# A solver round moved behind the value tiles, spare products inside the 64-row rounds, and an earlier forget product in a long one-core model kernel

## The chip, the cores and the metric

One core of a Trainium2 chip. The metric is the device time of one launch in microseconds (us), the median of the runs of a kernel. Everything is fp32.

## What is computed

A token sequence of 256 goes through two blocks of a model with D = 1024. Cut to what matters here:

```python
# first block: two layers; each: x += .5*norm(swiglu); x += norm(mixer); x += .5*norm(swiglu)
#   layer 0's mixer is an attention + state-space mixer, layer 1's is the RWKV-7 time mix
# second block, 16 meta tokens ahead of the 256, two of these "hybrid" layers:
def hybrid_layer(h, ...):
    u = rms_norm(h, norm_g)
    dq, dk, dv, dz, fq, fk, fv, fz, f_logit = split(u @ w_in)
    q1, q2, k1, k2 = rope(dq), ..., rope(dk), ...
    p = softmax(q1 k1) - lam * softmax(q2 k2)          # differential heads
    log_f = log_sigmoid(f_logit + b_forget); cum = cumsum(log_f)
    s = fq fk * scale + cum[query] - cum[key]          # forgetting heads
    return h + (concat(o_a * silu(dz), o_b * silu(fz)) @ w_out)
```

The RWKV time mix runs in two chunks of 128 tokens. Inside a chunk and a head it needs the inverse of a unit lower-triangular 128x128 matrix for each of 16 heads and 2 chunks. The 32x32 diagonal blocks are inverted on VectorE; the off-diagonal ones follow by products: one round that joins 32-blocks to 64-blocks, one that joins these to 128.

## The kernel before, in words

All engines run programs written out by hand in order; the order of issue on an engine is the order of the Python code, and semaphores tie the engines together. `product_pe`, `ffn_pe` and the projections are TensorE products of 128x128 weights; a helper `group` (line 277) issues the matmuls of one accumulation. In the trace each fp32 matmul is two MATMUL records. PSUM banks 0 to 3 are taken in turn by `turn_d` (VectorE empties them and raises `dve_out`), banks 4 to 7 by `turn_a` (ScalarE empties them, `act_out`); a turn n waits until turn n - 4 has been emptied. Weights come through a ring of six 1 MB slots. SyncE loads them in the order of `plan_weights`; slot n is loaded once slot n - 6 is released (`slot_used`), `take_slot` waits for its arrival.

**RWKV stage** (`rwkv_pe`, `rwkv_act`, `rwkv_dve`, `rwkv_pool`). On TensorE, in order: key, rate and eight receptance tiles (`r_product`, line 277) with the four pairs of score products (`pair_scores`, L1689) set among them; g1 and four value tiles; four groups of transposes "tok" (L1787) and the bonus product; four products `g2_product(t, h)` of two 512-column matmuls each; then the solver rounds. Round "m32" (L1815, 64 products of 32x32) needs `t64`, which VectorE copies at L2215 after its 31 steps of inversion (L2204, L2206). Round "t32" (L1828, L1830, 96 products of 32x32) needs m32 as emptied by VectorE (L2227, L2228) and the block-diagonal matrices `tts`, one copied by VectorE (L2221, `sc_dve` 2), one by ScalarE (L2054, `sc_act`). Rounds "m64" and "t64" (L1839, L1848) are 32 products of 64x64 each, in four groups of eight; each group is emptied by VectorE in 0.68 us. Then two small transposes `bonus_rows` (L1801), a drain, four full-array products of the identity with 512 columns of constants into one bank that nobody reads, and `chunk_pe`, the recurrence (L1896 to L1929). ScalarE empties tok, then g2 (`gtk`, L2049), then copies `tts[1]`.

**Hybrid stages** (`hybrid_pe` and its fellows). 32 feature tiles p = 0 to 31 in the order `FT`: dq0, dq1, dk0, dk1, dv0, dv1, dq2, ... Attention units (scores L2487, transposes L2499, value product L2513) are worked off from p = 5 on, one step of a unit beside each tile. ScalarE copies a tile out (L2542), GpSimd issues four DMAs per q or k tile that swap its halves (L2692, two buffers), VectorE does the rotation (L2632 to L2634) at step p + 2, and raises `roped`. A transpose of a value tile (L2472) waits until VectorE has copied the one before (L2639). At p = 11 TensorE does the forget product (8 columns, 16 records); VectorE adds the bias at step 11, ScalarE takes the logarithm at step 12, VectorE scans at step 13 (L2608). GpSimd, whose queue has all eight rotations ahead of it, then writes the sums to DRAM (L2694), reads them back to all partitions (L2696) and adds the masks (L2700). The first forgetting unit's scores need that.

**Mixer of layer 0** (`mixer_pe`). At p = 5 TensorE transposes the compressed probabilities (L1167), which VectorE has ready at L1552; ScalarE copies them (L1340) at its step 5. The first value product at p = 6 waits for that copy (`pct_done`).

```python
                    if u == 0:
                        pe.wait_ge(pct_done, 1)
```

Of the kernel before, what the change touches and what calls it, by code (L numbers as in the profile page):

```python
# [11 lines left out]
P = 128  # L12
S = 256
T = S // P
# [100 lines left out]
def plan_weights(d):  # L115
# [70 lines left out]
def model_kernel(nc, d, out, stop=None):  # L186
    ctx = ExitStack()
    with ctx:
# [853 lines left out]
        def mixer_pe(pe):  # L1042
# [74 lines left out]
            for p in range(STEPS):  # L1117
# [18 lines left out]
                if p == 2:  # L1136
# [26 lines left out]
                if p == 5:  # L1163
                    pe.wait_ge(pc_done, 1)
                    for t in range(T):
                        for g in range(2):
                            m = nc.tensor.transpose(ps[:, 7, (2 * t + g) * P:(2 * t + g + 1) * P],  # L1167
                                                    pcmp[:, t, 4 * g:4 * g + 4, :].rearrange("p h n -> p (h n)"), ident)
                    m.then_inc(pct_ready, 1)
# [108 lines left out]
        def mixer_act(act):  # L1278
# [35 lines left out]
            for p in range(STEPS):  # L1314
# [23 lines left out]
                if p == 5:  # L1338
# [320 lines left out]
        def rwkv_pe(pe):  # L1659
# [121 lines left out]
            s = S_V + 4  # L1781
            pe.wait_ge(krr, 3 * KD)
# [25 lines left out]
            g2_product(1, 1)  # L1808
            pe.wait_ge(sc_dve, 1)
            for t in range(T):  # L1810
                n = turn_d("m32", t)
                for h in range(SH):
                    ch = SH * t + h
                    for g in range(2):
                        m = nc.tensor.matmul(bank_d(n)[64 * g + 32:64 * g + 64, 32 * h:32 * h + 32],  # L1815
                                             at0[:, ch, :] if g == 0 else at64[64:96, ch, 32:64], t64[64 * g:64 * g + 32, ch, 0:32],
                                             start=True, stop=True, skip_group_check=True)
                m.then_inc(to_dve, 1)
            pe.wait_ge(sc_dve, 2)
            pe.wait_ge(sc_act, 1)  # L1820
            for t in range(T):
# [1001 lines left out]
```

## Time and profile before

| | us |
|---|---|
| median of 3 runs (1753.21 to 1759.9) | 1757.9 |
| the profiled execution, its time | 1766.56 |
| its span, first to last instruction | 1764.4 |
| TensorE busy in it | 1699.5 |
| granted TensorE clock, mean over the span | 0.984 |

Stages in the span: feed-forward 0 to 225, mixer 225 to 420, its output and two feed-forwards 420 to 870, RWKV stage 870 to 1130 (with its output product), feed-forward 1130 to 1340, hybrid 0 from 1340 to 1560, hybrid 1 from 1560 to the end. A clock of 1.00 in a row is 2.4 GHz, 0.50 is 1.2 GHz; a value between them is a stretch with some of each. Idle time in square brackets stands ahead of the instruction, with what ended it.

### The profile page before, as it was taken

Reading aid. Unit: us, or ns where it says so; the run is one execution under the profiler, and the core shown is the slowest. Engines: PE = TensorE matmul, PEld = TensorE weight load, DVE = VectorE, ACT = ScalarE, POOL = GpSimd, SP = SyncE. Lnnn points to the kernel's source line nnn. Section 1 sums busy time; section 2 is a strip of 40 time slices with the busy share of each in tenths; the row PEclk is TensorE's granted clock in tenths of the full one; section 3 lists DMA queues with packets and bytes.
Section 4 is the critical chain, followed back from the end, with each engine's and each line's share of the span. In section 5 each row is a group of like instructions: output and inputs, shape, how many; then the busy total and the mean of one; then the engine's idle time right before and its main releaser. Section 6 shows DMA issues by size and latency. Waiting matters only on the chain.

```text
span 1764.4 us, 26355 instructions
## 1 busy us (share of the span) xinstructions
PE 1699.5 (96%) x10798; PEld 1329.2 (75%) x10798; DVE 1033.8 (59%) x2001; ACT 420.3 (24%) x1049; POOL 260.0 (15%) x339
## 2 busy tenths in 40 slices
PE   8999999999999999999998999999998999999898
PEld 7997487775799749996476778699846777467674
DVE  5777435752577737776588647387754555325353
ACT  2000124532200002000157213201102344123431
POOL 3334000000022201221004040022201120011100
PEclk9999999999999999999999979999999999999999
DMA  8666744213454554545533300355557763468630
GB/s 263 216 210 206 170 109 138 73 53 107 132 176 159 191 169 141 178 157 191 143 103 119 120 25 2 98 189 165 176 144 150 119 119 106 79 108 120 118 111 24
DMA packets 196967, 237.27 MB, mean 134 GB/s; under 512 B 28300, under 2 KB 177216, under 8 KB 196592
## 3 DMA queue, kind: packets, MB, share of 16 engines
q1 hardware_dynamic: 191872, 224.97, 45.9%
q0 software_dynamic: 4960, 10.61, 1.9%
q8 instruction: 87, 1.43, 0.3%
q14 instruction: 32, 0.26, 0.0%
q10 hardware_dynamic: 16, 0.00, 0.0%
HBM read 232.30 MB, written 1.07 MB: 132 GB/s over the span
## 4 chain that ended last, share of the span: by engine, by line
PE 86%; DVE 6%; ACT 3%; DMA 2%; issue 2%; POOL 0%; POOLq 0%; SPq 0%; DVEq 0%; ACTq 0%
PE ps L589 28%; PE ps L277 23%; PE ps L655 14%; PE ps L518 6%; PE ps L599 3%; PE ps L1879 2%; DMA arena<-arena 1%; PE ps L2487 1%; PE ps L2499 1%; PE ps L2518 1%; PE ps L335 1%; DMA cum_rows<-arena 1%; PE ps L2513 1%; PE ps L1896 1%; PE ps L1702 0%
## 5 line engine op out<-in xcount | busy, mean ns | idle before, releaser
L277 PE MATMUL ps<-hT,ring 128*128 128x272 f32 (+4 forms) x1696 | 365.1, 372 | 4.3 <-ACT hT L359 4.0
L277 PEld LDWEIGHTS ps<-hT,ring 128*128 128x128 f32 (+1 forms) x1696 | 292.1, 193 | 59.6 <-issue 7.8
L589 PE MATMUL ps<-arena,ring 128*128 128x128 f32 x1280 | 162.6, 275 | 0.0
L655 PE MATMUL ps<-ring,arena 128*128 128x512 f32 x352 | 155.9, 593 | 1.7 <-DVE more L760 1.7
L850 POOL TENSOR_TENSOR arena<-arena 128x128 f32<-128x128 f32 x44 | 36.7, 833 | 793.4 <-DVE arena L774 449.7
L589 PEld LDWEIGHTS ps<-arena,ring 128*128 128x128 f32 x1280 | 152.6, 192 | 0.0
L589 PE MATMUL ps<-hT,ring 128*128 128x128 f32 x1280 | 150.1, 275 | 0.0
L589 PEld LDWEIGHTS ps<-hT,ring 128*128 128x128 f32 x1280 | 146.5, 192 | 0.0
L655 PEld LDWEIGHTS ps<-ring,arena 128*128 128x128 f32 x352 | 66.6, 190 | 87.1 <-issue 87.1
L589 PE MATMUL ps<-arena 128*128 128x128 f32 x960 | 120.3, 275 | 0.0
L589 PEld LDWEIGHTS ps<-arena 128*128 128x128 f32 x960 | 113.6, 192 | 0.0
L711 ACT ACTIVATE gains<-ps 128x512 f32<-128x512 f32 x40 | 23.9, 597 | 353.9 <-PE ps L589 353.9
L518 PE MATMUL ps<-ring,arena 128*128 128x512 f32 (+1 forms) x192 | 84.5, 596 | 0.7 <-ACT arena L2550 0.7
L783 DVE TENSOR_TENSOR gains<-gains,ps 128x256 f32<-128x256 f32 x40 | 16.8, 420 | 95.3 <-ACT gains L711 95.3
L518 PEld LDWEIGHTS ps<-ring,arena 128*128 128x128 f32 (+1 forms) x192 | 32.6, 174 | 50.1 <-issue 48.7
L2692 POOL DMA_DIRECT2D arena<-arena x64 | 31.4, 498 | 262.6 <-ACT arena L2542 238.7
L741 DVE TENSOR_TENSOR ring<-ring 128x512 f32<-128x512 f32 x80 | 70.1, 915 | 0.0
L655 PE MATMUL ps<-arena 128*128 128x512 f32 x144 | 65.8, 593 | 0.0
L599 PEld LDWEIGHTS ps<-hT,ring 128*128 128x128 f32 x512 | 60.4, 199 | 4.5 <-issue 4.3
L589 PE MATMUL ps<-hT,arena 128*128 128x128 f32 x480 | 63.4, 275 | 0.0
L599 PE MATMUL ps<-hT,ring 128*128 128x128 f32 x512 | 61.3, 283 | 2.0 <-DMA ring<-in_ffn_w_gate 1.5
L794 DVE TENSOR_TENSOR gains<-gains,ps 128x384 f32<-128x384 f32 x80 | 44.3, 554 | 27.0 <-PE ps L589 25.6
(488 smaller groups left out, 2720.4 us busy)
## 6 DMA issues: line engine op xcount, KB each, us to landing
ring<-in_ffn_w_gate SPq DMA_DIRECT2D x44, 1024.0 KB, 5.4
ring<-in_ffn_w_up SPq DMA_DIRECT2D x44, 1024.0 KB, 7.2
ring<-in_ffn_w_down SPq DMA_DIRECT2D x44, 1024.0 KB, 4.9
ring<-in_w_in SPq DMA_DIRECT2D x32, 1024.0 KB, 10.3
ring<-in_ab_w_in SPq DMA_DIRECT2D x12, 1024.0 KB, 5.3
ring<-in_w_out SPq DMA_DIRECT2D x8, 1024.0 KB, 5.0
ring<-in_ab_w_out SPq DMA_DIRECT2D x6, 1024.0 KB, 4.8
ring<-in_c_w_k SPq DMA_DIRECT2D x4, 1024.0 KB, 6.5
```

The lines of the kernel that those rows point to most:

```text
L277: last = nc.tensor.matmul(o, l, r, start=(i == 0), stop=(i == len(pairs) - 1))
L335: m = nc.tensor.transpose(ps[:, b + k // 4, (k % 4) * P:(k % 4 + 1) * P], xn[:, t, k * P:(k + 1) * P], ident)
L518: m = nc.tensor.matmul(o[:, h, :], lhs(k, t), slot2(n)[:, k % 2, h * 512:(h + 1) * 512], start=(k == 0), stop=(k == nk - 1))
L589: m = nc.tensor.matmul(o, left[:, k, :], right[:, k, :], start=(k == 0), stop=(k == 3))
L599: m = nc.tensor.matmul(ps[:, 4 + w, 256 * i + P * t:256 * i + P * (t + 1)], slot8(s0 + w)[:, k, i * P:(i + 1) * P], hT[:, k, h_cols(t)], s ...
L655: return nc.tensor.matmul(ps[:, BANK[i], :], hid[p][:, left, :], right, start=(p == 0), stop=(p == LAST))
L711: nc.scalar.activation(gu_e[:, :, 1:6:4], gu_a[:, :, 0:2], ACT.Copy).then_inc(a_copied, 1)
L741: nc.vector.tensor_tensor(w_part(n + w, 1, 0), w_part(n + w, 0, 0), w_part(n + w, 1, 0), ALU.subtract).then_inc(w_sums, 1)
L794: nc.vector.tensor_tensor(gu_e[:, w, 1:4], gu_e[:, w, 1:4], gu_b[:, w, 0:3], ALU.add).then_inc(b_taken, 1)
L850: nc.gpsimd.tensor_tensor(hid[q][:, 4], hid[q][:, 1], hid[q][:, 3], ALU.add).then_inc(hid_sums, 1)
L1879: m = nc.tensor.matmul(ps[:, 2 * t + h, :], yT[:, k, t * P:(t + 1) * P], slot2(s + k // 2)[:, k % 2, h * 512:(h + 1) * 512], start=(k == 0 ...
L2692: nc.gpsimd.dma_start(rth[to, (n - 1) % 2, fc], fmh[of, QK[kind] + i, fc]).then_inc(rot_in[(n - 1) % 2], 16)
```

## The change

**Mixer.** The transposes of the compressed probabilities go from the end of step 5 to the start of step 6, ahead of that step's scores; ScalarE's copy from step 5 to step 6.

**RWKV.** The receptance products come one earlier against the score products, on TensorE and on ScalarE. Round m32 is issued right behind the value tiles, and VectorE empties it before it makes `tts[0]`; ScalarE copies `tts[1]` ahead of emptying g2. Round t32 stands ahead of the last g2 product. A full-array product whose result nobody reads stands ahead of each of the eight groups of rounds m64 and t64; the four behind the rounds are gone.

**Hybrids.** The forget product and its chain on ScalarE and VectorE are four steps earlier (7, 8, 9), its weights stand fifth in the plan. The tile order begins dq0, dk0, dq1, dk1, and the first units wait for two rotations, not three; the first two slots are both released at p = 4. One activation table with both logarithm and exponential is loaded at the start of the stage.

```diff
 # plan_weights
-        for c in (0, 2, 4, 1, 3, 5, None, 8, 10, 12, 9, 11, 13, 6, 7, 14, 15):
+        for c in (0, 2, 4, 1, None, 3, 5, 8, 10, 12, 9, 11, 13, 6, 7, 14, 15):
 # mixer_pe, ahead of the scores of step p (behind them, with p == 5, before)
+                if p == 6:
+                    pe.wait_ge(pc_done, 1)
+                    for t in range(T):
+                        for g in range(2):
+                            m = nc.tensor.transpose(ps[:, 7, (2 * t + g) * P:(2 * t + g + 1) * P],
+                                                    pcmp[:, t, 4 * g:4 * g + 4, :].rearrange("p h n -> p (h n)"), ident)
+                    m.then_inc(pct_ready, 1)
 # mixer_act
-                if p == 5:
+                if p == 6:
                     act.wait_ge(pct_ready, 1)
 # rwkv_pe
-            for j in range(4):
+            for j in range(5):
                 r_product(j)
             pair_scores(0)
-            r_product(4)
+            r_product(5)
             pair_scores(1)
-            r_product(5)
+            r_product(6)
             pair_scores(2)
-            r_product(6)
+            r_product(7)
             pair_scores(3)
-            r_product(7)
...
             s = S_V + 4
+            pe.wait_ge(sc_dve, 1)
+            for t in range(T):
+                n = turn_d("m32", t)
...
             g2_product(0, 0)
             g2_product(0, 1)
             g2_product(1, 0)
-            g2_product(1, 1)
-            pe.wait_ge(sc_dve, 1)
-            for t in range(T):
-                n = turn_d("m32", t)
...
             pe.wait_ge(sc_dve, 2)
             pe.wait_ge(sc_act, 1)
...
+            g2_product(1, 1)
+            spare = pe_a.n + 1
+            pe.wait_ge(act_out, spare - 4)
+
+            def full_array():
+                group(bank_a(spare), [(ident, cst[:, 0:512])])
+
             for t in range(T):
                 pe.wait_ge(dve_out, job["t32", t])
                 for h8 in range(2):
+                    full_array()
                     n = turn_d("m64", t, h8)
...
                     pe.wait_ge(dve_out, job["m64", t, h8])
+                    full_array()
                     n = turn_d("t64", t, h8)
...
-            n = pe_a.n + 1
-            pe.wait_ge(act_out, n - 4)
-            for i in range(4):
-                group(bank_a(n), [(ident, cst[:, 0:512])])
 # rwkv_act: key_root(6), r_out(4), decays(5), key_root(7) now ahead of scores_out(0);
 #   r_out(6) ahead of scores_out(2), r_out(7) ahead of scores_out(3);
 #   the copies of tts[1] ahead of those of gtk
 # rwkv_dve: the copies of m32 right behind those of t64, ahead of those of tts[0]
 # the hybrids
+        FT[1], FT[2] = FT[2], FT[1]
...
-                      frees=p % 2 == 0).then_inc(f_ready, 1)
+                      frees=2 if p == 4 else 1 - p % 2).then_inc(f_ready, 1)
...
-                if p == 11:
+                if p == 7:
                     take_slot(pe, s)
                     x_turn()
...
-                        pe.wait_ge(roped, 8 * layer + (3, 4, 7, 8)[i])
+                        pe.wait_ge(roped, 8 * layer + (2, 4, 7, 8)[i])
 # hybrid_act
+            nc.scalar.preload_act_table_set(LN_EXP)
-                if p == 12:
+                if p == 8:
 # hybrid_dve: p == 11 becomes p == 7 (bias), p == 13 becomes p == 9 (scan)
```

## Rows read from the trace of the kernel before

**Rows 1.** The page: engine, busy us, share of the span, instructions.

```profile
PE 1699.5 (96%) x10798; PEld 1329.2 (75%) x10798; DVE 1033.8 (59%) x2001; ACT 420.3 (24%) x1049; POOL 260.0 (15%) x339
```

**Rows 2.** Stretches of 20 us: length, busy PE, PEld, DVE, ACT, POOL; clock, DMA share, GB/s.

```profile
300.00:320.00 20.00, 18.05 (x105) 14.44 (x106) 16.32 (x34) 9.95 (x31) 0.00 (x0) 0.91 0.18 53
...
940.00:960.00 20.00, 15.72 (x96) 12.60 (x95) 14.32 (x26) 19.26 (x58) 8.32 (x10) 0.91 0.31 106
...
1020.00:1040.00 20.00, 19.15 (x181) 16.42 (x182) 9.50 (x16) 0.00 (x0) 3.54 (x2) 0.50 0.16 52
...
1360.00:1380.00 20.00, 16.07 (x71) 12.05 (x70) 7.65 (x22) 2.97 (x12) 5.37 (x11) 0.91 0.55 103
...
1660.00:1680.00 20.00, 17.16 (x81) 13.32 (x82) 10.93 (x23) 8.71 (x21) 5.89 (x2) 0.83 0.43 81
```

**Rows 3.** Timeline, RWKV scores: start, us, engine, line, operation, idle before.

```profile
945.55 1.16 PE L1689 MATMUL ps<-gains,arena 64*128 64x128 f32 x16 [2.67 <-ACT more L1960]
...
962.44 1.25 DVE L2200 STREAM_TRANSPOSE arena<-arena 128x1024 f32<-128x1024 f32 x1 [1.15 <-ACT arena L1956]
```

**Rows 4.** Timeline from the value tiles to round t32.

```profile
970.27 27.89 PE L277 MATMUL ps<-ring,arena 128*128 128x256 f32 x128
...
991.84 3.20 DVE L2215 COPY gains<-arena 32x1024 f32<-32x1024 f32 x3
...
998.01 1.91 PE L1787 MATMUL ps<-cst,arena 128*128 128x128 f32 x16
...
1003.40 8.50 PE L277 MATMUL ps<-ring,gains 128*128 128x512 f32 x16
...
1012.43 4.28 ACT L2054 ACTIVATE arena<-arena 32x512 f32<-32x512 f32 x4
...
1016.81 0.26 PE L1828 MATMUL ps<-arena,more 32*32 32x32 f32 x2 [2.77 <-ACT arena L2054]
```

**Rows 5.** The chain that ended last, rounds m64, t64 and the four spare products.

```profile
1021.81 6.70 PE ps L1839 x61
...
1028.83 6.46 PE ps L1848 x61
...
1035.71 5.88 PE ps L277 x8
```

**Rows 6.** Timeline, VectorE ahead of the recurrence.

```profile
1036.47 0.91 DVE L2248 MEMSET gains<- 128x1024 f32 x1 [0.16 <-issue]
```

**Rows 7.** Timeline, mixer steps 5 and 6.

```profile
301.95 0.66 PE L1167 MATMUL ps<-cst,arena 128*128 128x128 f32 x4 [2.66 <-DVE arena L1552]
...
308.84 0.37 ACT L1321 ACTIVATE arena<-ps 128x256 f32<-128x256 f32 x1
...
309.19 2.82 PE L277 MATMUL ps<-arena 32*64 32x128 f32 x20
```

**Rows 8.** Timeline, hybrid 0: waits of TensorE and VectorE.

```profile
1367.38 0.22 PE L2487 MATMUL ps<-arena 64*16 64x16 f32 x4 [3.93 <-DVE arena L2634]
...
1365.84 0.44 DVE L2632 TENSOR_TENSOR arena<-arena,cst 128x272 f32<-128x272 f32 x1 [6.37 <-DMA arena<-arena]
...
1405.94 0.44 DVE L2632 TENSOR_TENSOR arena<-arena,cst 128x272 f32<-128x272 f32 x1 [2.49 <-DMA arena<-arena]
...
1432.18 5.96 DVE L2648 TENSOR_TENSOR arena<-arena 128x272 f32<-128x272 f32 x1
...
1433.07 4.76 POOL L2700 TENSOR_TENSOR gains<-gains,cst 128x2176 f32<-128x2176 f32 x1
```

**Rows 9.** Timeline, hybrid 1: the chain behind the forget product.

```profile
1635.95 0.52 POOL L2694 DMA_DIRECT2D cum_rows<-arena  x1 [21.74 <-DVE arena L2608]
...
1661.28 0.46 DVE L2624 TENSOR_TENSOR arena<-ps,more 128x288 f32<-128x288 f32 x1 [13.54 <-POOL more L2700]
...
1662.84 0.85 PE L2472 MATMUL ps<-cst,arena 128*96 128x128 f32 x3 [4.49 <-DVE arena L2639]
```

**Rows 10.** A stretch in hybrid 1 behind its second wait, columns as in rows 2.

```profile
1662.90:1668.20 5.30, 5.30 (x18) 3.87 (x19) 5.23 (x7) 0.53 (x3) 2.99 (x1) 0.50 0.07 23
```

More of the change, by code:

```diff
@@ L1781, in rwkv_pe @@
             s = S_V + 4
+            pe.wait_ge(sc_dve, 1)
+            for t in range(T):
+                n = turn_d("m32", t)
+                for h in range(SH):
+                    ch = SH * t + h
+                    for g in range(2):
+                        m = nc.tensor.matmul(bank_d(n)[64 * g + 32:64 * g + 64, 32 * h:32 * h + 32],
+                                             at0[:, ch, :] if g == 0 else at64[64:96, ch, 32:64], t64[64 * g:64 * g + 32, ch, 0:32],
+                                             start=True, stop=True, skip_group_check=True)
+                m.then_inc(to_dve, 1)
             pe.wait_ge(krr, 3 * KD)
@@ L2046, in rwkv_act @@
                     nc.scalar.activation((btk, ktk)[w][:, j4 * 512:(j4 + 1) * 512], next_a(), ACT.Copy).then_inc(act_out, 1)
-            for t in range(T):
-                for h in range(2):
-                    nc.scalar.activation(gtk[:, t, h * 512:(h + 1) * 512], next_a(), ACT.Copy).then_inc(act_out, 1)
             act.wait_ge(solved, 1)
@@ L2055, in rwkv_act @@
             m.then_inc(sc_act, 1)
+            for t in range(T):
+                for h in range(2):
+                    nc.scalar.activation(gtk[:, t, h * 512:(h + 1) * 512], next_a(), ACT.Copy).then_inc(act_out, 1)
             nc.scalar.preload_act_table_set(LN_EXP)
@@ L2217, in rwkv_dve @@
                     m.then_inc(sc_dve, 1)
+            for t in range(T):
+                b = next_d().rearrange("p (h n) -> p h n", h=SH)
+                cs = slice(SH * t, SH * t + SH)
+                nc.vector.tensor_copy(m32[32:64, cs, :], b[32:64])
+                nc.vector.tensor_copy(m32[96:P, cs, :], b[96:P]).then_inc(dve_out, 1)
             dve.wait_ge(tt_zero, 3)
@@ L2223, in rwkv_dve @@
             nc.vector.tensor_copy(bsum, next_d()[64:80, 0:S]).then_inc(dve_out, 1)
-            for t in range(T):
-                b = next_d().rearrange("p (h n) -> p h n", h=SH)
-                cs = slice(SH * t, SH * t + SH)
-                nc.vector.tensor_copy(m32[32:64, cs, :], b[32:64])
-                nc.vector.tensor_copy(m32[96:P, cs, :], b[96:P]).then_inc(dve_out, 1)
             for t in range(T):
@@ L2436, in hybrid_pe @@
             for p in range(4):
-                if p % 2 == 0:
-                    take_slot(pe, s + p // 2)
+                if p < 2:
+                    take_slot(pe, s + p)
                 raw_n[FT[p]] = n = f_turn()
                 fc = slice(f_cols(layer, FT[p][0]).start, META + P)
-                group(f_bank(layer, n)[:, fc], [(slot8(s + p // 2)[:, k, (p % 2) * P:(p % 2 + 1) * P], hT[:, k, fc]) for k in range(KD)])
+                group(f_bank(layer, n)[:, fc], [(slot8(s + p % 2)[:, k, (p // 2) * P:(p // 2 + 1) * P], hT[:, k, fc]) for k in range(KD)])
             trans_pe(pe, 1)
@@ L2444, in hybrid_pe @@
             for p in range(4):
-                if p == 2:
-                    s += 1
                 fc = slice(META + P, L2)
-                group(f_bank(layer, raw_n[FT[p]])[:, fc], [(slot8(s)[:, k, (p % 2) * P:(p % 2 + 1) * P], hT[:, k, fc]) for k in range(KD)],
-                      frees=p == 2).then_inc(f_ready, 1)
-            s += 1
+                group(f_bank(layer, raw_n[FT[p]])[:, fc],
+                      [(slot8(s + p % 2)[:, k, (p // 2) * P:(p // 2 + 1) * P], hT[:, k, fc]) for k in range(KD)]).then_inc(f_ready, 1)
+            s += 2
             for p in range(4, len(FT)):
```

32 lines of the change are left out of this document (9 added, 23 removed).

## The prediction

> **What bounds the kernel.** I read the page first: TensorE is busy for 96% of the span [rows 1]. So the end moves only by what TensorE gets rid of: its own work, its idle gaps, and the time that it works at half clock. The table of 20 us stretches shows where the last two lie [rows 2]. In nearly all stretches TensorE is busy for 20 of 20 us at clock 1.00; the rows shown are exceptions, and each lies where the change works. 0.91 is 3.4 to 3.6 us at 1.2 GHz, 0.83 is 6.8 us, and from 1020 to 1040 all of it. Then I read the timeline around each exception, for what ended the wait.
>
> In the RWKV solver the chain of events is plain [rows 4]. Tok starts at 998.0, the four g2 products end at 1011.9, round m32 ends at 1014.04 (1016.81 less 2.77). Then TensorE waits 2.77 us for ScalarE, whose copy of `tts[1]` began only after g2 was emptied and took 4.28 us. In this wait, behind 2 us of 32-row products, the clock fell. It stayed at 1.2 GHz through both 64-row rounds, 13.3 us of dense work [rows 5], and rose only inside the full-array products behind them: at half clock a 512-column product takes about 1.7 us, at full clock at most 1.06 (8.50 / 8, [rows 4]), and the four took 5.88. The recurrence starts at 1041.6.
>
> **The change, part by part.** Times are against the profiled execution.
>
> *Solver.* From the start of tok (or now m32) to the recurrence, before: 1041.6 - 998.0 = 43.6 us. After, all at full clock: m32 2.1 (1014.04 - 1011.9); tok 1.9; bonus product 3.5 (1003.40 - 998.01 - 1.91); four g2 8.5; t32 3.2 (m32's 2.1 for 64 products, times 96/64); 64-row rounds half of 6.70 + 6.46, 6.6; eight spare products at 1.06, 8.5; bonus_rows and drain 0.5. The sum is 34.8. The spare product's 0.85 to 1.06: I take the g2 row, since it too changes between kinds of tile. Two changes of tile per group instead of one could add 0.1 each, 0.8 in all.
>
> Is anything late in this order? m32 needs the second copy of `t64`, 992 + 2.1 = 994, and the value tiles end at 998.0: 4 us of cover, where before 18 us of g2 and others lay between. If VectorE's inversion began 4 us later, each further us would count in full. `tts[1]` now starts on ScalarE behind tok (about 5 us in) and is done 9.3 us in; t32 comes 16 us in. VectorE empties m32 and makes `tts[0]` by 7. Each group of a round is emptied in 0.68 us beside about 1.9 of TensorE. All hidden. Ahead of the recurrence VectorE clears a state for 0.91 us, until 1037.4, 1.8 us behind bonus_rows [rows 6]; the four spare products hid that. With none behind, the first emptying comes about 0.9 late. Solver: -8.8 + 0.9 = **-7.9**, between -10.5 (spare products at 0.85, memset hidden) and -5 (changes of tile dear).
>
> *Receptance against scores.* ScalarE is the bound there, 19.26 of 20 us busy [rows 2], TensorE waits for it, 2.67 us at the most [rows 3]. Done by hand in the new order: TensorE has r_product(7), 3.5 us, ahead of its last wait and not behind it. ScalarE has one more copy and the later waits ahead of the last scores, so that VectorE's inversion starts some 1.7 us later than 962.4; the value tiles end 0.7 us earlier. So m32's 4 us of cover shrink to 1.6. I take **-0.5**, from -2.5 to +2.
>
> *Mixer.* The 2.66 us wait for VectorE at 301.95 goes [rows 7]; the tile of step 6 fills it, and the half clock behind it (0.09 of 20 us, 1.8) goes too. But ScalarE's copy is now in its step 6, behind the exponentials and the convolution's sigmoid of step 5, which wait for VectorE; its step 6 began at 308.84. The copy ends at 309.8 (308.84 + 0.37 + some 0.6 for 512 columns), and the first value product, at 309.19 before, starts there. Worked forward from the tile before, TensorE has done its scores by about 306.3 (VectorE's mask of the unit before decides) and then has nothing for 3.5 us, longer than the wait that went, so the clock falls again, now over products and a tile of some 6 us. Sum: +0.6, and 0 to +3.6 for the clock. **+2**, from +0.5 to +4. No copy or wait behind it gives it back, since TensorE is dense after.
>
> *Hybrids, first units.* TensorE waited 3.93 us in hybrid 0 for the third rotation [rows 8] and a little less in hybrid 1; each was followed by 3.4 us of half clock. VectorE in turn waited 6.37 for its DMA. With two rotations needed, the score product goes ahead, but the third rotation is as late as it was, and VectorE's order has it ahead of the first unit's mask and of the copy of the first value tile, for which TensorE waits one tile later (by about 2.4 us). The earlier forget product, 3.6 us, is moved, not added. The later wait for it, 0.7, goes. The step 11 rotation also came by a late DMA, at 1405.94; TensorE, now 3 us ahead, would run into it. And both first slots are released together, so 2 MB of weights are in the queues when the third rotation is issued. I take **-2.5** and **-1**, from -5 to +3 each.
>
> Of this the Trainium skill, "DMA: Bandwidth & Descriptors", section "Queues, rings and completion order", says that each engine takes turns between queues at the granularity of a packet. By that rule a small rotation DMA would hardly wait for a ring load, and both terms would be at their good end, about -5. The 6.37 us wait disagrees as far as it goes.
>
> *Hybrid 1, bias.* The chain from the scan takes 1661.2 - 1635.95 = 25 us [rows 9], and VectorE waits 13.54 for it. Four steps earlier (about 5 us each, 32 tiles in some 160 us), and with GpSimd's eighth rotation issued by 1614.2 (1635.95 less 21.74), it starts some 20 us sooner, so the 13.54 are covered with 6 or more to spare. TensorE's 4.49 go, and the half clock behind it, 5.3 us of dense work at half rate, 2.7 [rows 10]. **-7.2**, from -8 to -5.
>
> *Bias additions elsewhere.* GpSimd's 4.76 us held VectorE's L2648 up to 5.96 us where its like takes 0.44 [rows 8]. They fall 20 us earlier now, beside units of the differential heads in both hybrids. In hybrid 0 this cost a TensorE gap of about 2 us and half clock before, and will again. In hybrid 1 it is new, in a looser stretch. **+1**, from 0 to +4.
>
> The skill, "SBUF — State Buffer", section "Who interferes with whom", says that a VectorE instruction with two SBUF inputs waits for a GpSimd one that reads SBUF to its end. The row agrees. It speaks against the move: the whole 4.76 us and more of stall in each hybrid, the +4 end.
>
> *Tables.* The table loads inside the hybrids fall away. ScalarE is 24% busy over the span [rows 1], no TensorE wait shown ends on one. 0.
>
> Sum: -7.9 - 0.5 + 2 - 2.5 - 1 - 7.2 + 1 = -16.1. The profiled execution, 1766.6, is 8.7 above the median; 1750.5 there is **1742** on the median's scale.
>
> **Rivals.**
>
> *Stalls move (0.24).* The late DMAs and VectorE's order hold TensorE in both hybrids: +2.5 and +1 in place of -2.5 and -1 would be net +7 on the sum, the mixer at +4, 2 more. -16.1 + 9 = -7: 1751. For it: every wait there ends on a DMA whose landing is not moved. Against: hybrid 1's bias gap is large and simple.
>
> *The solver gains half (0.08).* m32, with 1.6 us of cover, waits for `t64`, and tile changes cost 0.2 a piece: -4 in place of -7.9: 1746, and with part of the first rival 1750.
>
> *Slower: the clock falls in t32 and nothing lifts it (0.06).* The trace has it fall behind 32-row work and not rise through 13.3 us of 64-row work [rows 5]. If t32's 3.2 us between g2 products let it fall, g2 costs 2.1 more, the rounds 6.6 more, the spare products 5 to 7 more: +14.7, which alone only gives 1757. But with no dense block behind, the recurrence begins at half clock; if its first 26 us are done so, they add up to 22: 1779. It decides from there: up to the recurrence it is no change, beyond it slower. Against: full-array products stand in each group, and the clock held through 8.5 us of g2 and m32 before the idle wait.
>
> **How the numbers follow.** Likeliest 0.62, own range 1735 to 1750; the rivals as above. 0.5% is 8.8 us, about what a measurement of this kernel can tell: faster below 1749.1, slower above 1766.7. Faster: nearly all of the first case, 0.60, a quarter of the second, half of the third: 0.69. Slower: the clock case and a little: 0.07. Same 0.24. The range leaves out the clock case and the ends: 1733 to 1756.
>
> **What the profile would show.** Clock 1.00 all through the solver, no wait ahead of L1828, 35 us from value tiles to recurrence, and about 1 us ahead of the first L1908. The mixer's gap moves from L1167 to the first value product. In hybrid 1 no wait for L2700; some gap at the second L2472 of each hybrid. The prediction is wrong if the clock dips in t32, if the rotations land later than before, or if spare products and rounds take over 18 us.

## The result

The changed kernel takes **1781.5 us** (1779.3 to 1781.9), the kernel before 1757.9: slower by 1.1%, ratio 1.0108 [1.0076, 1.0141]; the two medians by themselves would give 1.3%, inside that interval. The forecast was faster, 1742, with at most 1756. What came is close in time to the rival to which I gave 0.06 (1779), and its first half is what happened; its second half, a recurrence begun at half clock for 26 us, did not in the profiled execution. That the two times agree is therefore luck: mixer and hybrids, slower than that sum had them, made up for it.

### The profile after

The page first, then the 20 us stretches that answer to [rows 1, 2]. Columns: stretch, its length, busy time of TensorE, its weight loads, VectorE, ScalarE and GpSimd, granted clock, DMA share, GB/s.

```profile
PE 1711.2 (96%) x10806; PEld 1330.9 (75%) x10806; DVE 1036.0 (58%) x2001; ACT 394.6 (22%) x1029; POOL 260.1 (15%) x339
```

```profile
300.00:320.00 20.00, 15.07 (x75) 12.11 (x75) 13.12 (x30) 9.65 (x31) 0.00 (x0) 0.83 0.17 53
940.00:960.00 20.00, 14.26 (x77) 11.54 (x76) 17.39 (x29) 15.59 (x47) 11.06 (x14) 0.87 0.27 84
1000.00:1020.00 20.00, 18.67 (x337) 11.08 (x336) 8.70 (x14) 8.60 (x12) 1.80 (x1) 0.99 0.22 73
1020.00:1040.00 20.00, 19.91 (x114) 10.47 (x114) 4.37 (x7) 1.88 (x2) 0.00 (x0) 0.50 0.01 2
1040.00:1060.00 20.00, 19.74 (x107) 12.83 (x105) 5.85 (x11) 0.00 (x0) 2.56 (x2) 0.50 0.10 31
1380.00:1400.00 20.00, 12.31 (x53) 8.31 (x50) 6.13 (x20) 2.32 (x11) 3.25 (x7) 0.83 0.90 153
1600.00:1620.00 20.00, 11.99 (x52) 8.68 (x52) 7.66 (x20) 2.78 (x11) 1.96 (x4) 0.83 0.94 156
1660.00:1680.00 20.00, 20.00 (x102) 15.57 (x101) 11.60 (x22) 5.61 (x18) 7.56 (x2) 1.00 0.77 166
```

TensorE is as busy as before, 96%, but busy longer: 11.7 us more. The eight spare products and four taken away can't explain that at full clock. The stretch at half clock is now two rows of 20 us where it was one. The hybrids' sore points have moved: the last row, hybrid 1's wait for the sums, is whole and at full clock, as forecast, and two new rows near 1390 and 1610 have lost 8 us each.

By stage, from the starts of the same products in the two traces (spans 1764.4 and 1777.5): mixer +3.4 us, scores +1.5, value tiles to recurrence +10.4 (43.5 to 53.9), recurrence +1.2, hybrid 0 -0.4, hybrid 1 -3.1: 13.0. That is against a profiled execution of before that stood 8.7 above the median of its runs. The profiled execution of after is 2.2 us below the median of its runs, so the timed difference, 19 us by the ratio and 23.6 by the medians, is larger than the 13 of the profiles.

TensorE through the solver, to be held against [rows 4, 5]:

```profile
1020.09 0.26 PE L1826 MATMUL ps<-arena,more 32*32 32x32 f32 x2 [1.42 <-issue]
1020.98 4.08 PE L277 MATMUL ps<-ring,gains 128*128 128x512 f32 x4
1024.99 2.08 PE L277 MATMUL ps<-cst 128*128 128x512 f32 x2
1026.99 1.97 PE L1845 MATMUL ps<-gains,hT 64*64 64x64 f32 x16
...
1052.29 2.07 PE L277 MATMUL ps<-cst 128*128 128x512 f32 x2
1054.29 1.97 PE L1855 MATMUL ps<-arena,gains 64*64 64x64 f32 x16
...
1059.70 1.00 PE L1911 MATMUL ps<-arena 128*128 128x64 f32 x4
...
1061.50 0.66 PE L1911 MATMUL ps<-arena 128*128 128x64 f32 x4
```

The wait for ScalarE at t32 is gone. In its place, near the end of t32's 192 records, TensorE stops for 1.42 us, from 1018.7, for nothing that an engine did ("issue"). Just as it stopped a 16 KB block came in on the queue that carries instructions, alone on the DMA engines:

```profile
q8 instruction: 1, 0.02, 1.3%
```

It began at 1017.9 and took 1.0 us; TensorE went on 1.2 us behind its landing. All thirteen kernels whose profile has such a stop agree: it lasts 0.44 to 2.18 us, and TensorE goes on 1.2 to 1.5 us behind the landing of a block, in the kernel before as well. That TensorE ran out of instructions and waited for this block is inferred from that, not shown. The clock fell at 1019.5, in the stop. From there each g2 product, spare product and round runs at half rate: a spare product 2.0 from start to start, a group 1.9, eight times 3.9. None of the eight full-array products lifted the clock, nor did all of them together. It rose at 1060.4, 3.6 us into the recurrence: the same four products take 1.00 us before and 0.66 behind.

Mixer and scores, for [rows 7] and [rows 3]; each wait is followed by 6.8 us at half clock:

```profile
303.61 0.60 PE L1153 MATMUL ps<-cst,arena 128*128 128x128 f32 x4
305.69 0.72 PE L1167 MATMUL ps<-arena 64*128 64x128 f32 x8 [1.48 <-DVE arena L1508]
309.85 5.07 PE L277 MATMUL ps<-arena 32*64 32x128 f32 x20 [3.44 <-ACT arena L1340]
```

```profile
953.57 1.16 PE L1689 MATMUL ps<-gains,arena 64*128 64x128 f32 x16 [4.31 <-DVE gains L2195]
```

Hybrid 0, for [rows 8]: TensorE, then VectorE's third rotation, GpSimd's issue of its transfers, and SyncE's loads:

```profile
1391.65 0.85 PE L2474 MATMUL ps<-cst,arena 128*96 128x128 f32 x3 [7.69 <-DVE arena L2642]
```

```profile
1388.05 0.44 DVE L2635 TENSOR_TENSOR arena<-arena,cst 128x272 f32<-128x272 f32 x1 [11.82 <-DMA arena<-arena]
```

```profile
1372.88 1.96 POOL L2695 DMA_DIRECT2D arena<-arena  x4 [1.26 <-ACT arena L2545]
```

```profile
1372.77 8.37 SPq L308 DMA_DIRECT2D ring<-in_w_in  x3
```

The third rotation's transfers were issued 0.1 us behind a 1 MB load and landed 15.2 us later, where it was 8.3 before [rows 8]: 1365.84 less 1357.57, the latter GpSimd's issue in the trace of before. A second 1 MB load went out at 1373.2, among these transfers. Hybrid 1 shows the same with 8.0 us of wait.

### The profile page after: what moved, and what is told of

It reads as the page before. It is cut to its first block, busy times and chain, and to the rows that moved or that the text cites. A ratio compares the mean times of both kernels' runs of the same rounds, so it can differ in the third digit from the quotient of the medians.

```text
span 1777.5 us, 26346 instructions
## 1 busy us (share of the span) xinstructions
PE 1711.2 (96%) x10806; PEld 1330.9 (75%) x10806; DVE 1036.0 (58%) x2001; ACT 394.6 (22%) x1029; POOL 260.1 (15%) x339
## 4 chain that ended last, share of the span: by engine, by line
PE 88%; DVE 6%; ACT 2%; DMA 2%; issue 1%; POOL 0%; SPq 0%; DVEq 0%; ACTq 0%
PE ps L589 28%; PE ps L277 25%; PE ps L655 14%; PE ps L518 6%; PE ps L599 3%; PE ps L1882 2%; DMA arena<-arena 2%; PE ps L2489 1%; PE ps L2501 1%; PE ps L2520 1%; PE ps L335 1%; PE ps L2515 1%; PE ps L1899 1%; PE ps L1702 0%; DMA ring<-in_ffn_w_gate 0%
## 5 line engine op out<-in xcount | busy, mean ns | idle before, releaser
L277 PE MATMUL ps<-hT,ring 128*128 128x272 f32 (+4 forms) x1696 | 358.4, 367 | 4.3 <-ACT hT L359 4.0
L277 PEld LDWEIGHTS ps<-hT,ring 128*128 128x128 f32 (+1 forms) x1696 | 287.2, 190 | 58.0 <-issue 8.1
```

What stands on the lines that cost most here:

```text
L277: last = nc.tensor.matmul(o, l, r, start=(i == 0), stop=(i == len(pairs) - 1))
```

## The experiments

Ratios are to the kernel before on the same chip, whose median was 1760 to 1761 in all sets. Where the executions of a kernel fall into two groups, the ratio lies nearer to that of the means than to that of the medians.

### Which part cost what

**a_rwkv, a_hybrids, b_mixer, d_scores**: the kernel before with one part of the diff alone. d_scores takes from the RWKV part only the order of receptance and scores.

> The kernel before with the RWKV part of the change alone (order of receptance and scores, m32 early, t32 ahead of the last g2, spare products inside). By the two profiles that stage grew by 13.1 us: 1.5 in the scores, 10.3 from value tiles to recurrence, 1.2 in the recurrence's first products at half clock. If the parts don't touch one another, this kernel is 13 us slower than before (1.0075). Rival: part of it came from the stage's later start behind the mixer (3.4 us); then it is 8 us or less.

> The kernel before with the hybrid part of the change alone. By the two profiles hybrid 0 is 0.4 us shorter and hybrid 1 3.1 us, so the time falls by 3.5 us (0.998), with a wait of nearly 8 us for the third rotation at the second value tile of both. Rival: these waits were made by the phase at which the stage began; then they are 4 us or less here, and the time falls by 10 us.

> The kernel before with the mixer part of the change alone. By the two profiles TensorE's wait of 2.66 us ahead of the transposes became one of 3.44 at the first value product, with 6.8 us at half clock behind it for 3.4: 3.4 us slower up to the mixer's output. Theory: that is its whole effect, 3 to 4 us slower (1.002). Rival: the wait is taken back later in the mixer where TensorE waits for others; then no difference.

> The kernel before with the new order of receptance and score products alone. By the two profiles it costs 1.5 us up to the value tiles (a wait of 4.3 us in place of 2.7, 6.8 us at half clock in place of 3.4, less 0.75 and 0.85 of smaller waits). Nothing behind it takes that back: 1 to 2 us slower. Rival: the later start of VectorE's inversion costs nothing either, so it is within 1 us of before.

```
            median us   ratio to before
a_rwkv      1774.3      1.0078 [1.0049, 1.0108]
b_mixer     1765.6      1.0024 [1.0008, 1.0040]
a_hybrids   1764.5      1.0014 [0.9997, 1.0031]
d_scores    1760.8      1.0004 [0.9982, 1.0025]
```

The three parts sum to 1.0116, the change measured 1.0108: they account for all of it. The RWKV part is two thirds of the loss. The profiled execution of a_rwkv shows how deep it can go: t32's stop, 1.44 us, and behind it the clock low through the rounds and through the whole first half of the recurrence, until 1101.3.

```profile
1015.21 0.22 PE L1826 MATMUL ps<-arena,more 32*32 32x32 f32 x2 [1.44 <-issue]
```

```profile
1016.00:1101.00 85.00, 84.74 (x416) 65.75 (x417) 21.34 (x46) 8.53 (x26) 17.86 (x8) 0.50 0.04 13
```

That execution took 1792.9 us, the others 1770.6 to 1775.6. The mixer behaves as its profile said. The scores' 1.5 us can't be told from nothing. The hybrids' part, which by the profiles gains 3.5, does not gain in the timed runs. Waits of 7.7 us at the second value tile stand in both hybrids here too, so they don't come from the stage's start time.

### What fells the clock, and what lifts it

**a_behind**: no product inside the rounds, four behind them again. **b_batches**: as many as in the change, but four ahead of the first 64-row group and four behind the last.

```diff
 # a_behind
-                    full_array()
...
+            for i in range(4):
+                group(bank_a(n), [(ident, cst[:, 0:512])])
 # b_batches: besides, the same lines behind g2_product(1, 1)
```

> The changed kernel without the eight full-array products inside the rounds, and with the four behind the rounds, as in the kernel before. Theory 1 (the products inside lift nothing): the clock falls in t32 as before and stays low through g2(1,1) and the rounds, 4.0 + 13.2 us, and rises inside the four behind, 5.9 us; the stretch from m32 to the recurrence is 17.5 + 4.0 + 13.2 + 0.5 + 5.9 = about 41 us instead of 53.9, the recurrence starts at full clock, and the time falls by 13 to 15 us. Rival: the 16 us that eight spare products take at half clock are not lost, because without them each group waits for VectorE to empty the one before (0.68 us and its way); then the rounds take 18 us or more and the time falls by less than 10.

> The changed kernel with its eight full-array products in two batches: four ahead of the first 64-row group, four behind the last, none inside the rounds. Theory: a full-array product among 64-row groups doesn't lift a fallen clock, four in a row do (the kernel before rose inside its four). Then the clock rises in the first batch (5.9 us), the rounds run at full clock in 6.6 us and the second batch in 4.2, and the stretch from m32 to the recurrence is 17.5 + 4.0 + 5.9 + 6.6 + 0.5 + 4.2 = about 39 us for 53.9; the time is 13 to 17 us below the changed kernel's. Rival: 64-row products bring the clock down again by themselves; then the rounds take 10 to 13 us and the second batch 5.9, 45 us or more, and the time is 5 to 9 us below.

a_behind: 1769.9 us, 1.0039 [1.0023, 1.0055], 11.6 below the changed kernel (13 to 15 expected); value tiles to recurrence 42.0 us. So spare products inside the rounds are pure cost once the clock is down. b_batches lifted the clock in the first batch as expected, and the rounds behind it stayed at full clock; the stretch took 39.8 us (39 expected). Stretches of b_batches, the last in the recurrence:

```profile
1021.00:1031.00 10.00, 8.65 (x51) 3.51 (x51) 2.77 (x5) 1.88 (x2) 0.00 (x0) 0.50 0.01 2
1031.20:1044.20 13.00, 12.89 (x142) 9.38 (x140) 6.68 (x11) 0.00 (x0) 2.73 (x2) 1.00 0.19 55
1075.60:1119.80 44.20, 44.20 (x223) 41.98 (x224) 26.80 (x68) 9.88 (x37) 0.00 (x0) 0.50 0.00 1
```

But its time is 1784.8 us, 1.0104 [1.0066, 1.0142], no better than the changed kernel: 3 of 10 executions at 1763 to 1770, 7 at 1784 to 1788. The last row is why, in the one that was profiled. Both theories missed it.

**a_split**: the changed kernel with the last g2 product between the halves of t32. **e_mix**: the changed kernel with all four g2 products spread.

```diff
 # a_split, in the loop over t of round t32
-            g2_product(1, 1)
+                if t == 0:
+                    g2_product(1, 1)
 # e_mix: g2_product(0, 0) ahead of t32, then
+                if t == 1:
+                    g2_product(0, 1)
 # and in the loop over t of round m64
+                g2_product(1, t)
```

> The changed kernel with its last g2 product issued between the two halves of round t32 and not behind both; nothing else differs. Theory 1 (the fall is t32's): in the changed kernel TensorE stopped for 1.42 us inside t32, until a 16 KB instruction transfer had landed, and the clock fell in that stop. With a 2 us product of full width in that place the stop is covered, the clock holds, and the stretch from m32 to the recurrence goes from 53.9 us to about 35; the time falls by 18 us or so, to within 0.3% of the kernel before. Rival: the clock falls anyway, one or two groups later, because eight full-array products among 64-row groups are too thin to hold it; then the stretch is 48 to 52 us and the time falls by less than 6 us.

> The changed kernel with everything as it is but the place of the four g2 products: one ahead of each half of t32, one ahead of each half of m64 (in the changed kernel three ahead of t32 and one behind it; in a_split one of them was moved between the halves). The eight products inside the rounds stay. Theory (the run of thin rounds and their waits, unbroken by other work, is what the clock fell in): the stretch from m32 to the recurrence is 35 us, as d_inside's, in all executions; the time is 17 to 22 us below the changed kernel's 1781, near the kernel before. Rival 1 (the order of receptance, or the later start of everything behind the mixer, has a part in the fall): two kinds of executions as in a_split, the median above 1770. Rival 2 (what is left above before is in mixer and hybrids): then it stays 5 to 8 us above the kernel before less 7 of the solver's gain, about 1760.

The solver came out as expected in both, 35.9 us at full clock, without the stop in t32:

```profile
1005.14:1041.01 35.87, 35.61 (x516) 20.49 (x515) 14.95 (x23) 10.51 (x14) 1.80 (x1) 1.00 0.10 31
```

The times did not. a_split: 1779.6 us, 1.0077 [1.0045, 1.0110], with 3 of 10 executions at 1762 to 1766 (one of these was profiled) and 7 at 1779 to 1783. e_mix: 1779.9 us, 1.0084 [1.0050, 1.0118], one of 6 at 1763.9, five at 1779 to 1782. My theory of a_split, that t32 is the only place of a fall, fell with it, and so did that of e_mix, that the run of thin rounds is. The profiled execution of e_mix is one of the five, and shows the place: TensorE's wait where the recurrence passes from the first chunk to the second, and the stretches around it.

```profile
1071.04 0.74 PE L1909 MATMUL ps<-gains 128*128 128x128 f32 x2 [1.08 <-DVE arena L2259]
```

```profile
1020.00:1040.00 20.00, 19.74 (x162) 11.63 (x162) 5.78 (x11) 2.20 (x3) 0.09 (x1) 1.00 0.00 1
1071.20:1115.50 44.30, 44.30 (x223) 41.86 (x224) 26.71 (x68) 10.07 (x38) 0.00 (x0) 0.50 0.00 1
1115.60:1125.00 9.40, 9.40 (x24) 4.14 (x23) 1.27 (x3) 0.25 (x2) 0.00 (x0) 1.00 0.01 2
```

The clock falls there and stays down for the 44 us of the second chunk, though TensorE is never idle in them; it rises at the output products of 512 columns behind it. That is up to 22 us.

**c_solver**: the kernel before, with m32 behind the value tiles, `tts[1]` copied ahead of emptying tok, the g2 products spread as in e_mix, VectorE's order as in the change, and the four spare products behind, as before. The mixer, the scores and the hybrids are those of before. **d_inside**: the same with eight inside and none behind. **d_none**: with none at all.

> The kernel before with the solver alone reordered, and no product inside the rounds: m32 behind the value tiles; ScalarE copies tts[1] ahead of tok; the four g2 products stand ahead of t32's first half, ahead of its second, and ahead of each half of m64; the four spare products stay behind the rounds. Theory (the clock is what matters, and mixed with g2 it holds): m32 2.1, tok 1.9, bonus 3.5, g2 8.5, t32 3.2, rounds 6.6, bonus_rows 0.5, spare products 4.2: 30.5 us from value tiles to recurrence instead of 43.6, 13 us faster. Rival: the clock falls here too in a part of the executions, as in the changed kernel with its round t32 split, and then the same stretch costs 40 to 45 us; then executions of two kinds, some 13 us below and some at or above the kernel before, and the median says which is commoner.

> c_solver with the eight full-array products inside the rounds, one ahead of each group, and none behind, as the change has it. Theory 1 (the place of t32 was the fault, not these products): with the four g2 products among the rounds the clock holds, eight products of 0.95 to 1.05 us replace four, the stretch grows by some 3.5 to 4 us, and VectorE's clearing of the state, no longer covered, adds 0.9: 4 to 5 us slower than c_solver, 7 below before. Rival (with nothing dense behind the rounds the recurrence starts thin, and the clock falls there in a part of the executions): two kinds of executions, one as above, one 15 to 20 us slower, the median 5 to 10 us above the kernel before.

> c_solver without any spare product. If they are needed only to lift a clock that has fallen, and it doesn't fall here, the stretch is 4.2 us shorter and 0.9 us comes back as a wait for VectorE: 3 us faster than c_solver, 15 below before. Rival as in d_inside: without dense work between rounds and recurrence the clock falls there, in a part of the executions, for 15 us or more.

```
            median us (range)          ratio to before           solver us
c_solver    1749.3 (1747.6 to 1756.0)  0.9932 [0.9907, 0.9957]   29.9
d_inside    1754.0 (1747.8 to 1762.0)  0.9959 [0.9939, 0.9979]   35.9
d_none      1746.1 (1739.7 to 1762.0)  0.9910 [0.9886, 0.9935]   26.4
```

All three ran their solver at clock 1.00; this is d_none's:

```profile
998.18:1024.59 26.41, 26.15 (x499) 17.50 (x499) 14.95 (x23) 10.60 (x14) 1.80 (x1) 1.00 0.14 42
```

The same round t32 and the same eight spare products as in the change are harmless here. With real products among the thin rounds no spare one is needed, 17 us of 43.5 go, and 15 of them are in the time. Only one of d_none's 12 executions, at 1762.0 with a mean clock of 0.980 (the others 0.990 to 0.994), looks like a fall of e_mix's kind, and none of 12 of d_inside. No run spreads the g2 products alone; but a_behind, which has m32 early, `tts[1]` sooner and no wait for ScalarE, and not the spreading, still took 42.0 us there, 12 more than c_solver.

What these runs do not separate is the stop from the thin work around it. Every kernel without the stop also has a g2 product between the halves of t32, and either may be what holds the clock. In the profiles of the change, a_behind and b_batches the clock falls inside the stop, in that of a_rwkv 0.8 us behind its end.

### The hybrids

**b_forget**: the kernel before with the forget chain and its place in the plan alone. **c_keep**: the same, but the plan as before. **b_apart**: the hybrid part with the two slots released one by one.

```diff
 # c_keep, tile 7; the slot's own release is counted at tile 12
-                    take_slot(pe, s)
+                    take_slot(pe, s + 2)
 # b_apart, second halves of tiles 0 to 3
+                      frees=p == 3).then_inc(f_ready, 1)
```

> The kernel before with the forget product and its chain four steps sooner (and its table loaded at the start of the stage) alone; the order of tiles, the first units' wait and the release of slots stay as before. Theory: this half of the hybrid part is the good one. The 13.5 us that VectorE waited for the sums in hybrid 1 go, TensorE's 4.5 us with them and 2 to 3 us at half clock; its 0.7 us ahead of the forget product too. 5 to 8 us faster. Rival: the masks' additions on GpSimd now fall beside VectorE's work in both stages and cost as much; then within 3 us of before.

> The kernel before with the forget product and its chain four steps sooner, as in b_forget, but with the order of loads left as it was: the product reads its slot (the seventh of the stage) at tile 7, two slots ahead of its turn, and the slot is released in its turn. Theory (the plan's order did the harm): with the 32 KB of forget weights moved to the fifth place, a 1 MB load takes their place at the first release of the stage, 1352.3 us, just as the rotations are issued, and the first units waited 10.2 and 9.3 us for them, 3.9 and 3.1 before. With the old order these waits stay at 3 to 4, hybrid 1's wait of 4.5 us for the sums goes with the half clock behind it, and the time is 5 to 8 us below the kernel before (0.996). Rival: the sooner chain itself holds the rotations (VectorE, GpSimd); then the waits are near 10 us again and it is 5 us or more slower than before.

> The hybrid part of the change alone, with its first two slots released one by one (the first at the second half of tile 3, the second at tile 4), where the change releases both at tile 4. Theory (two 1 MB loads in the queues at once starve the small rotation transfers): with both released together the third rotation's transfers, issued at 1372.9 in the changed kernel, landed 15 us later, against 8.3 before. Released apart by one tile (4 to 5 us), the first load is nearly through when the second starts; the rotation lands 4 to 7 us sooner, the waits of 7.7 us at the second value tile shrink to 1 to 4, and the time falls by 8 to 13 us against the hybrid part as it stands, to some 8 us below the kernel before. Rival: any ring load delays them alike, and the third rotation waits for the same 2 MB either way; then the waits stay above 6 us and the time moves by less than 3.

b_forget: 1768.0 us, 1.0045 [1.0031, 1.0058]. I had taken it for the good half; it is slower than the whole hybrid part. TensorE waits 10.20 us at the first unit of hybrid 0, 9.25 in hybrid 1:

```profile
1373.52 0.24 PE L2487 MATMUL ps<-arena 64*16 64x16 f32 x4 [10.20 <-DVE arena L2635]
```

```profile
1352.33 4.18 SPq L308 DMA_DIRECT2D ring<-in_w_in  x2
```

The tile order, the units' wait and the releases are those of before. What differs at that moment is which load goes out at the first release. In the kernel before it is the 32 KB of forget weights, 2.9 us from issue to landing; with these moved to fifth in the plan it is the 1 MB of column block 5, 14.8 us from issue to landing. c_keep confirms it: with the old plan the first units wait 3.74 and 3.66 us, for 3.93 and 3.1 before. But its time is 1770.3, 1.0047 [1.0029, 1.0066], and its profile has another wait that was not there, and its like in hybrid 1 (3.79 us):

```profile
1411.02 0.50 PE L2473 MATMUL ps<-cst,arena 128*96 128x128 f32 x3 [4.24 <-DVE arena L2641]
```

In the kernel before the forget product, 3.6 us of TensorE's work, stood at tile 11, just ahead of the value tile that needs the eighth rotation, and hid its late transfers: issued at 1390.5, they let VectorE go on at 1405.94 [rows 8], and TensorE came to that value tile at 1407.95 without a wait; its one wait near there, 0.68, was for the bias addition. In c_keep they are as slow, issued at 1393.9 and in at 1409.0, but TensorE is there by 1406.8. Moved to tile 7, the forget product hides nothing there, and the 4.2 us and 6.8 at half clock behind them cost what hybrid 1's wait for the sums gave. b_apart: 1771.6, 1.0061 [1.0037, 1.0085], with waits of 6.17 and 6.35 in hybrid 0 and 5.7 and 1.0 in hybrid 1; the load released sooner caught the second rotation also. Releasing the two slots together was thus not the fault, against my expectation; the 1 MB load at that moment is.

**c_late**: the kernel before with the second slot released at tile 6 together with the third. **c_both**: c_keep and this. **d_best**: c_both and c_solver. **e_best**: c_both and d_none.

```diff
 # c_late; in c_both also 12: 2
-                      frees=p % 2 == 0).then_inc(f_ready, 1)
+                      frees={4: 0, 6: 2}.get(p, 1 - p % 2)).then_inc(f_ready, 1)
```

> The kernel before with the second slot of a hybrid released at tile 6 together with the third, not at tile 4; nothing else. Theory: in the kernel before a 1 MB load was issued 1.3 us ahead of the third rotation's transfers, which landed 8.3 us later, 4 after issue without one. With the load held back until the rotations are in, the waits of 3.9 and 3.1 us at the first units go, with half clock behind them: 5 to 9 us faster. Rival: the two loads then meet the fifth and sixth rotations, and what is gained is given back; within 3 us.

> Both of these together. Theory: their waits are different ones, so the gains add up, 10 to 15 us faster than before (0.993). Rival: the loads held back meet the fifth and sixth rotations, for which VectorE, three units ahead of the forget chain, waits; then no better than c_keep alone.

> c_solver and c_both together: 11.7 and 1.2 us below before by their medians, so 12 to 14 us faster than before (0.9925) if they don't touch one another. Rival: the hybrids' gain was of the size of the measurement's noise; then it equals c_solver's 0.9932.

> d_none and c_both together: solver mixed with g2 and no spare products, forget product sooner with the plan of before, the second slot's release held back. By their medians 14.7 and 1.2 us below before: 15 to 17 us faster (0.991) if they add up. Rival: the hybrids' part is no gain and the time equals d_none's, 0.991 within 2 us, or the clock falls at the recurrence in some executions, as in one of 12 of d_none.

```
            median us (range)          ratio to before
c_late      1763.9 (1758.7 to 1771.0)  1.0011 [0.9989, 1.0033]
c_both      1759.7 (1758.5 to 1762.7)  0.9985 [0.9967, 1.0003]
d_best      1748.7 (1746.5 to 1750.8)  0.9922 [0.9900, 0.9943]
e_best      1744.9 (1744.1 to 1746.7)  0.9904 [0.9887, 0.9922]
```

c_late takes the waits at the first units away (none in hybrid 0, 1.2 us in hybrid 1), and gets new ones, 3.9 us in hybrid 0 and 3.3 in hybrid 1, behind VectorE's wait for the seventh rotation (7.1 us in hybrid 0): the rival. c_both shows no gain against before that can be told from none. Against c_keep, on the same chip, it is 10.6 us faster, so holding the load back pays once the forget product has moved; c_both's rival, no better than c_keep, did not come. d_best can't be told from c_solver. **e_best** is 16 us faster than the kernel before and 36 faster than the changed one, nearly all of it d_none's; the part of the hybrids in it is not shown.

## Why the prediction was wrong

*What bounds the kernel.* Right: idle gaps and the clock decided it. Between the forecast's sum, -16.1, and the +13.0 of the profiles lie 29.1 us: 19.5 of them in the solver with the recurrence behind it, 2.0 in the scores, 1.4 in the mixer, 6.2 in the hybrids.

*Solver.* The step that failed is "After, all at full clock", which made -7.9 of what measured +11.6. The sum of the pieces was sound: 34.8 us forecast, 35.9 measured in a_split, e_mix and d_inside, where the clock held (the rounds took 8.6 for 6.6, the rest a little less than forecast). In the changed kernel it fell in t32, and the same work took 53.9. I gave this 0.06 and argued against it from two things. "Full-array products stand in each group": they do, and at half clock they lift nothing in 31 us. "The clock held ... before the idle wait": so it did, but I took the wait for ScalarE for the only one. The kernel before has a second stop in t32, 1.1 us put down to issue, at 1019.7 to 1020.8, with an instruction block on the queue from 1018.5:

```profile
1020.75 0.26 PE L1828 MATMUL ps<-arena,more 32*32 32x32 f32 x1 [1.09 <-issue]
```

The clock was down already, so it seemed free. It is the one that stayed when the other went. Of the rival's own terms, against e_mix at full clock, g2 (1.9 more, for 2.1) and the rounds (6.6 more, as priced) held; the spare products cost 7.5 more (for 5 to 7), and the stop 1.4 that the rival did not have. The recurrence's first 26 us did not come true in the changed kernel: 3.6 us at half clock, for 1.2. They did in one of the nine executions of a_rwkv, 1792.9 us.

*m32's cover.* It held: in the changed kernel `t64` was ready 2.7 us before m32 began (1.6 forecast), and m32 waited for nothing in any run.

*Scores.* -0.5 forecast, +1.5 in the profile, inside its bounds, not measurable in time.

*Mixer.* +2 forecast, from 0.5 to 4; +3.4 by the profile, with the wait at the place named and 3.44 us long (3.5 forecast). The clock's part came out near its upper bound: 6.8 us at half clock are 3.4 lost (at most 3.6).

*Hybrids, first units.* -2.5 and -1 forecast, each at most +3. The wait moved to the second value tile, the place named, but took 7.7 and 8.0. The step said that "the third rotation is as late as it was"; it was 15.2 us behind its issue and not 8.3. I had seen 2 MB in the queues and priced only the release, not that the plan's new order puts a 1 MB load where 32 KB had been.

The Trainium skill's rule of turns per packet ("DMA: Bandwidth & Descriptors", section "Queues, rings and completion order") had given -5 for this. The measurement is far off on the other side: four transfers of 34 KB took 15.2 us beside two loads of 1 MB. The profile records such a load in pieces of 1 KB; if the rule's packet holds many of them both may be true, but no run here shows how many.

*Hybrid 1, bias.* The wait for the sums went, all of it, and the stretch at 1660 is at clock 1.00, where it was 0.50 [rows 10]. -7.2 was its price in the profiled execution of before, which stood 8.7 above the median. I subtracted the 8.7 as a constant, while part of what the change removes may be what makes an execution stand above the others; that is not shown. In timed runs the hybrid part gained nothing. *The moved forget product* was costed at nothing, as moved and not added; c_keep shows that where it stood it covered 3.6 us of a late rotation.

*Bias additions.* VectorE's stall is 6.81 us in hybrid 0 now, and TensorE waits for none of it: 0 where +1 was forecast. "SBUF — State Buffer", section "Who interferes with whom", of the Trainium skill is right on the stall; it was the cover that I undersized.

**What stays open.** Why e_mix, a_split and b_batches mostly fall at the recurrence's second chunk while the kernel before, c_solver and d_inside don't, although the instructions there, the 1.08 us wait in most of them and the clock ahead of it are alike. The first three have the mixer, score and hybrid parts of the change, the others don't; the hybrids lie behind the place. Those parts can't be all of it, for the changed kernel and a_behind have them too, and neither the profile nor the spread of their times (3 us each) shows such a fall. e_mix and d_inside also differ in ScalarE's order: e_mix copies `tts[1]` behind emptying tok, d_inside ahead of it. Nor do I know where a_split loses 17 us in seven of its ten executions: the one profiled was not among them.

## What to carry to other kernels

Spread thin work among real dense work before buying spare products: a solver with four g2 products between its rounds was 12 to 15 us faster, and eight spare ones, behind a fallen clock, took 16 and lifted nothing. It did not help in every setting: with the rest of the change around it (e_mix) the clock fell later in most executions. Before a product or a load is moved, ask what it hides and what takes its place: a 3.6 us product covered a late transfer, and a 32 KB load kept a 1 MB one away from the rotations. When a wait at a clock's fall is removed, read on for the next idle stretch behind it, however cheap it looks at half clock.

## What was not expected of the hardware

- A round of 192 records of 32-row products stops near its end for 0.4 to 2.2 us, until 1.2 to 1.5 us behind the landing of a 16 KB block on the instruction queue. The stop was 1.4 to 2.2 us where the round ran at full clock and 0.4 to 1.15 where it ran at half; with a g2 product between the halves of the round it was gone. That TensorE waits for instructions there is the likely reading.
- A granted clock of 0.50 lasts through 44 us of a TensorE that is never idle, if its work is the recurrence's; four 512-column full-array products in a row lifted it (before, a_behind, b_batches), eight with 64-row groups between them did not.
- One kernel's executions can differ by 17 us or more: 1763.9 and 1781.6 in e_mix with the same instructions, at mean clocks of 0.989 and 0.976.
- The loads of `w_in` differ by which 256 columns they fetch. In the kernel before, from issue to landing, blocks 8, 10 and 12 took 8.1 to 10.3 us in both hybrids, blocks 9 and 13 14.3 to 15.8, and block 5 14.6 and 14.8 in the changed kernel and in b_forget. Blocks 8 and 9 of hybrid 0:

```profile
ring<-in_w_in SPq DMA_DIRECT2D x1, 1024.0 KB, 8.8
...
ring<-in_w_in SPq DMA_DIRECT2D x1, 1024.0 KB, 15.5
```

  The numbers of the costly blocks (5, 9, 13) are 1 modulo 4. What makes them so was not tried. The eighth rotation's slow transfers, in the kernel before and in c_keep, also ran beside a load of block 9.
